# Hybrid recurrent decoder step: sample states stored between weight requests, and x and the first root placed first

## The chip, the cores and the metric

The kernel runs on one core of a Trainium2 chip. The metric is the time of one execution on the device, in microseconds (us); the numbers are medians over several runs.

## What is computed

One step of a decoder trunk of one layer with D = 1024, for a prompt of 512 tokens and a sample group of 8 sequences of 4 tokens. The kernel holds both as one tile of 544 columns. The reference, cut to what matters:

```python
mod = silu(c) @ ada_w + ada_b                    # adaLN, 6 x 1024 per group
h   = rms(x, norm1_w) * (1 + sc1) + sh1
proj = h @ w_in                                  # one projection for four mixers and their gates
# A: gated delta rule, B: HGRN2, C: SSD, D: mLSTM; each scans chunks and carries a state
o_a, S_gdn  = gated_delta(q, k, v, beta, logd, S_gdn)
o_b, S_hgrn = hgrn2(silu(q), kg, v, logf, S_hgrn)
o_c, S_ssd  = ssd_scan(C, B, x * dt, dt * -exp(a_log), S_ssd)      # then * silu(s_z)
o_d, C, n, m = mlstm(q, k, v, ig, lf, C, n, m)
y = (sum_n sigmoid(gate_n) * (branch_n @ w_branch_n)) @ w_out
x = x + gt1 * y
x = x + gt2 * (swiglu(rms(x, norm2_w) * (1 + sc2) + sh2))
return rms(x, final_norm_w), all new states of prompt and sample
```

The prompt's states start at zero. Those of the sample group are inputs, and their new values are outputs: `state_gdn`, `state_hgrn` and `state_mlstm_c` of 8 x 4 x 64 x 64 and `state_ssd` of 8 x 8 x 64 x 32 in float32, and some small ones.

## The kernel before, in words

Work goes to five instruction streams that wait for each other through semaphores. TensorE (PE) multiplies, ScalarE (ACT) copies PSUM out, takes exponentials and splits weights into a high part, VectorE (DVE) makes the low parts and the rest of the elementwise work, GpSimd (POOL) clears a few tiles, and SyncE (SP) asks for nearly every DMA, in one queue. SyncE's instructions run in program order, and one that waits for a semaphore holds up every request behind it.

**Opening.** SyncE requests c, the constants (`cst`, with the identity), x of the prompt and of the sample, four adaLN weights, small vectors, four more adaLN weights (L614 to L618 and after). TensorE first transposes c (stage `ct`); that needs the constants and c after its silu (stage `silc`, L1677). VectorE copies the result (`ctc`, L2007). Then TensorE transposes x in eight steps d; for each, ScalarE copies PSUM to `xT0` (L1687), VectorE squares (L2027) and TensorE sums the squares with a matrix of ones (`first_squares`, into banks 4 and 5). Between them it multiplies silu(c) with the first adaLN weights (`first_rows`) and turns the rows of the result into columns (`turn_rows`, 16 records in the profile for two of them, two records to a multiplication). The root, x's reciprocal norm, is a logarithm (L1697) and an exponential (L1699) on ScalarE, the stage `rs1`. After it VectorE normalises x (L2054), ScalarE makes high parts (L1725) and VectorE low parts (L2082) of h, for k = 0 to 7. Then VectorE makes the low part of the small gate weights (L2136).

**Mix stage.** 13 groups of `w_in` of 256 columns, two tiles each, are multiplied with h, each tile in four parts of 12 products. 22 tiles come early; the tiles 22 and 23 (SZ, written over Q_s, the SSD states of the sample) and 24 and 25 (MO) come after eight adaLN units. The weights lie in a ring of four slots, and `loads` numbers the requests: 0 to 3 and 15 to 30 are adaLN, 4 to 14 and 31, 32 mix, 33, 34 the two z groups. Request n waits until the work on request n - 4 is done. An adaLN unit v takes two requests, 15 + 2v and 16 + 2v (L634 for all of them). ScalarE copies each finished half tile out of PSUM (L1741) and makes the weights' high parts (`weights_high`, L1713); VectorE the low parts (`weights_low`, L2061).

**Chains.** Into this work the stages of three chains are woven: gdn (delta rule), hgrn, and rest (SSD, then mLSTM), each over the prompt's tiles and once over the sample's (t = NT). The order of all four is computed by `shared_order` from a table of costs, and fixed; each engine runs its part of it in that order. The stage `s_statec` finishes the sample's SSD states in Q_s, `g_statec` those of the delta rule in Q_g, `h_statec` those of HGRN2 in Q_h. They are sums made by VectorE (L2305). Q_s, Q_g and Q_h lie in `pj`, where later the tiles SZ, GZ and HG are written, so these writes wait for the stores, for instance

```python
if f == SZ:
    act.wait_ge(q_out["ssd"], 128)
act.activation(pj[:, f, h * HN:(h + 1) * HN], ps[:, h, 0:HN], ACT.Copy).then_inc(x_read, 1)
```

Q_c, the mLSTM states, lies where SSD's B and C were; it is fetched after `s_statec` (L729) and read by the sample's stage `m_out`. After the last of the 35 requests SyncE fetches Q_c, stores Q_s and S_s (the prompt's SSD state, L733), then Q_g and Q_h (L744). The gate weights follow.

Of the kernel before, what the change touches and what calls it, by code (L numbers as in the profile page):

```python
# [56 lines left out]
Y_BANK = [6, 0, 2, 6, 0]  # L57
ADA_ORDER = [0, 1, 4, 5, 2, 3, 6, 7]
# [312 lines left out]
def trunk(nc, A, O):  # L371

    ctx = ExitStack()
    with ctx:
# [237 lines left out]
        def _(sp):  # L612

            sp.dma_start(ctok(pj)[0:1, :], A["c_prompt"]).then_inc(d_c, 16)  # L614
            sp.dma_start(ctok(pj)[1:NB + 1, :], A["c_sample"]).then_inc(d_c, 16)
            sp.dma_start(cst[:, :], A["const"]).then_inc(d_cst, 16)
            sp.dma_start(xtok(pj), A["x_prompt"][0].rearrange("(a p) d -> p a d", p=P)).then_inc(d_x, 16)
            sp.dma_start(xstok(pj), A["x_sample"].rearrange("b t d -> (b t) d")).then_inc(d_x, 16)  # L618
# [79 lines left out]

            for n in range(R + 2, len(loads)):
# [6 lines left out]
                load(kind, n % R, idx)  # L706
                if n == 7:

                    pre.after(sp, 0, "xc")
                    sp.dma_start(x_out, part(0, KD * TA)).then_inc(d_xout, 16)  # L710
                    sp.dma_start(s_hist[0:3 * NB, :], A["state_ssd_conv"][0].rearrange("b k c -> (b k) c")).then_inc(d_hist, 16)
                    pre.after(sp, 0, "norm1")
                    sp.wait_ge(d_xout, 16)
                    sp.dma_start(g_hist[0:3 * NB, :], A["state_gdn_conv"][0].rearrange("b k c -> (b k) c")).then_inc(d_hist, 16)
# [11 lines left out]
            rest.after(sp, NT, "s_statec")  # L726
            for p in range(2):
                for q in range(2):
                    sp.dma_start(Q_c[q * DK:(q + 1) * DK, p], A["state_mlstm_c"][0, :, 2 * p + q].rearrange("b k v -> k b v")).then_inc(d_q["mlstm"], 16)  # L729
            stored_at = [0]  # L730

            def store(dst, src):
                sp.dma_start(dst, src).then_inc(stored, 16)  # L733
                stored_at[0] += 16

            def heads(dst, S):
                for p in range(2):
                    for q in range(2):
                        store(dst[2 * p + q], S[q * DK:(q + 1) * DK, p])

            def qheads(dst, S, name):
                for p in range(2):
                    for q in range(2):
                        sp.dma_start(dst[:, 2 * p + q].rearrange("b k v -> k b v"), S[q * DK:(q + 1) * DK, p]).then_inc(q_out[name], 16)  # L744
# [6 lines left out]
            for g in range(2):  # L751
                for j in range(4):
                    sp.dma_start(O[13][0, :, 4 * g + j].rearrange("b n v -> n b v"), Qs(Q_s)[g * DK:(g + 1) * DK, j]).then_inc(q_out["ssd"], 16)
                    store(O[5][0, 0, 4 * g + j], S_s[g * DK:(g + 1) * DK, j])
            gdn.after(sp, NT, "g_statec")
            qheads(O[10][0], Q_g, "gdn")
            hgrn.after(sp, NT, "h_statec")
            qheads(O[12][0], Q_h, "hgrn")
# [87 lines left out]
        def _(pe):  # L846
# [46 lines left out]
            for d in range(KD):  # L893
# [7 lines left out]
                if d in (1, 3, 5, 6):  # L901
                    first_rows((1, 3, 5, 6).index(d))
            first_squares(KD - 1).then_inc(x_summed, 1)
            turn_rows(0)
# [769 lines left out]
        def _(act):  # L1674
# [39 lines left out]

            for e in range(2):
                weights_high(0, e)
            act.wait_ge(x_summed, 1)
            rsqrt(pre, "rs1", two(rstd[:, :]), ps[:, 4:6, 0:HN], 1.0 / D)
# [269 lines left out]
        def _(dve):  # L1988
# [77 lines left out]
            for e in range(2):  # L2066
                weights_low(0, e)
            pre.after(dve, 0, "rs1")
            for k0 in (0, 4):
# [8 lines left out]
                for k in range(k0, k0 + 4):  # L2078
                    if k < k0 + 3:
# [3 lines left out]
                                             in1=h_hi[:, k, 0:T].bitcast(F32), op0=ADD, op1=SUB).then_inc(h_split, 1)  # L2083

# [862 lines left out]
```

## Time and profile before

| | us |
|---|---|
| median of 3 runs | 1234.47 |
| lowest and highest of them | 1229.53, 1234.59 |
| the profiled execution, its own time | 1237.73 |
| its span in the profile | 1235.9 |
| TensorE busy in it | 1162.4 |
| VectorE busy | 576.2 |
| ScalarE busy | 396.7 |

The profile is of one execution. Its times are counted from the start of the span, so the time of the program is the span and 1.8 us around it. Busy TensorE time is time with at least one matmul in flight; matmuls overlap, so the duration of one is longer than the distance between two starts. "PEclk" is the granted clock of TensorE as a share of 2.4 GHz; it has two levels, 1.2 and 2.4 GHz.

### The profile page before, as it was taken

The page shows a single profiled execution, that of the slowest core. Times are in us where ns is not written, and L with a number is a line of the kernel's source. Part 1 is how long each engine was busy: PE and PEld are TensorE (multiplying, and loading weights), DVE is VectorE, ACT ScalarE, POOL GpSimd, SP SyncE. Part 2 cuts the span into 40 slices and gives each one's busy share as a digit, 9 for nine tenths or more (in the row PEclk, how much of TensorE's full clock was granted, in tenths as well). Part 3 has the DMA queues.
Part 4 walks back from the last instruction along what each step waited for, and adds up shares of the span by engine and source line. Part 5 has one row for each costly group of instructions (what it writes and reads, how often), then busy time and mean ns, then how long its engine had stood idle before and what let it go on. Part 6 is the DMA issues. An engine that isn't in the chain of part 4 may idle for free. (4 is left out here: it accounts for less than half of the span.)

```text
span 1235.9 us, 26871 instructions
## 1 busy us (share of the span) xinstructions
PE 1162.4 (94%) x11789; PEld 1086.7 (88%) x11789; DVE 576.2 (47%) x1035; ACT 396.7 (32%) x546; POOL 11.6 (1%) x29
## 2 busy tenths in 40 slices
PE   6789989998989889999999999879999999999997
PEld 3589978887667879999999989779999999999996
DVE  1657867778578453523333354452222222453332
ACT  2535577521012136722222211242222232331121
POOL 0001100000000000000000000000000000000000
PEclk9889999998689799999999999989999999999998
DMA  9915311113646343363333231312323332232301
GB/s 297 278 49 118 109 36 37 37 37 105 206 139 170 75 102 79 84 141 86 85 86 86 86 86 39 97 35 69 102 75 95 88 82 81 70 94 72 94 1 73
DMA packets 191033, 116.76 MB, mean 94 GB/s; under 512 B 36650, under 2 KB 189351, under 8 KB 190678
## 3 DMA queue, kind: packets, MB, share of 16 engines
q1 hardware_dynamic: 190358, 115.16, 33.4%
q8 instruction: 79, 1.29, 0.4%
q0 software_dynamic: 576, 0.14, 0.1%
q14 instruction: 20, 0.16, 0.0%
HBM read 108.31 MB, written 6.96 MB: 93 GB/s over the span
## 5 line engine op out<-in xcount | busy, mean ns | idle before, releaser
L848 PE MATMUL ps<-high_parts,scr_parts 128*128 128x272 f32 x2848 | 549.8, 292 | 13.0 <-DVE hT_parts L2813 7.0
L848 PEld LDWEIGHTS ps<-high_parts,scr_parts 128*128 128x128 f32 x2848 | 452.8, 190 | 16.5 <-issue 7.7
L848 PE MATMUL ps<-hT_parts,scr_parts 128*128 128x272 f32 x1488 | 413.4, 290 | 0.0
L2710 DVE TENSOR_TENSOR scr_parts<-ring,scr_parts 128x1024 fp32r<-128x1024 f32 (+1 forms) x104 | 133.7, 1286 | 330.1 <-ACT scr_parts L1872 327.4
L848 PEld LDWEIGHTS ps<-hT_parts,scr_parts 128*128 128x128 f32 x1488 | 276.0, 189 | 0.0
L1872 ACT ACTIVATE scr_parts<-ring 128x1024 fp32r<-128x1024 f32 (+1 forms) x104 | 115.2, 1108 | 464.5 <-PE ps L848 464.1
L848 PE MATMUL ps<-pj_parts,scr_parts 128*128 128x272 f32 x992 | 166.5, 292 | 2.1 <-DVEq L2012 1.8
L848 PEld LDWEIGHTS ps<-pj_parts,scr_parts 128*128 128x128 f32 x992 | 140.5, 188 | 3.6 <-DVEq L2012 2.2
L848 PE MATMUL ps<-high_parts,ring_parts 128*128 128x272 f32 x416 | 124.2, 299 | 0.0
L848 PEld LDWEIGHTS ps<-high_parts,ring_parts 128*128 128x128 f32 x416 | 82.9, 199 | 0.1
L848 PE MATMUL ps<-scr 64*64 64x64 f32 (+6 forms) x2352 | 80.5, 233 | 2.4 <-DVEq L2012 1.3
L848 PEld LDWEIGHTS ps<-scr 64*64 64x64 f32 (+3 forms) x2352 | 63.6, 136 | 15.6 <-issue 7.0
L848 PE MATMUL ps<-high_parts,wx_hi 128*128 128x272 f32 x224 | 70.1, 313 | 6.1 <-ACT pj L1741 3.8
L848 PE MATMUL ps<-hT_parts,wx_hi 128*128 128x272 f32 x224 | 66.6, 297 | 0.0
L848 PE MATMUL ps<-high_parts,pj_parts 128*128 128x272 f32 x192 | 60.6, 315 | 3.3 <-ACT pj L1741 3.3
L848 PE MATMUL ps<-hT_parts,pj_parts 128*128 128x272 f32 x192 | 57.2, 298 | 0.0
L848 PEld LDWEIGHTS ps<-high_parts,wx_hi 128*128 128x128 f32 x224 | 44.5, 199 | 8.8 <-ACT pj L1741 4.6
L848 PEld LDWEIGHTS ps<-hT_parts,wx_hi 128*128 128x128 f32 x224 | 44.4, 198 | 0.0
L848 PEld LDWEIGHTS ps<-high_parts,pj_parts 128*128 128x128 f32 x192 | 38.2, 199 | 5.6 <-ACT pj L1741 3.9
L1741 ACT ACTIVATE pj<-ps 128x272 f32<-128x272 f32 x52 | 20.2, 389 | 66.9 <-PE ps L848 57.0
L2762 DVE TENSOR_TENSOR Rr<-pj,ps 128x544 f32<-128x544 f32 x16 | 11.5, 721 | 63.3 <-PE ps L848 63.0
L848 PE MATMUL ps<-pj 64*64 64x64 f32 (+2 forms) x308 | 37.8, 309 | 3.2 <-ACT scr L1853 3.2
(332 smaller groups left out, 1193.3 us busy)
## 6 DMA issues: line engine op xcount, KB each, us to landing
ring<-in_w_in_dram SPq DMA_DIRECT2D x62, 512.0 KB, 5.5
ring<-in_ffn_w_in_dram SPq DMA_DIRECT2D x44, 512.0 KB, 5.1
ring<-in_ada_w_dram SPq DMA_DIRECT2D x40, 512.0 KB, 6.1
ring<-in_ffn_w_out_dram SPq DMA_DIRECT2D x16, 384.0 KB, 3.6
ring<-in_ffn_w_out_dram SPq DMA_DIRECT2D x16, 320.0 KB, 4.1
pj<-in_ada_w_dram SPq DMA_DIRECT2D x8, 512.0 KB, 8.1
ring<-in_w_out_dram SPq DMA_DIRECT2D x8, 512.0 KB, 6.4
x_scratch<-scr SPq DMA_DIRECT2D x1, 2176.0 KB, 12.0
```

The source lines that it names most:

```text
L848: return pe.matmul(out, lhsT, rhs, start=start, stop=stop, skip_group_check=True)
L1741: act.activation(pj[:, f, h * HN:(h + 1) * HN], ps[:, h, 0:HN], ACT.Copy).then_inc(x_read, 1)
L1872: act.activation(hi, src, ACT.Copy).then_inc(w_split_hi, 1)
L2710: dve.tensor_tensor(lo, src, hi.bitcast(F32), SUB).then_inc(w_split, 1)
L2762: dve.tensor_tensor(two(Rr[:, :]), gate_t, lift, MUL).then_inc(lin_read, 1)
```

## The change

Four things are moved and nothing is added or left out:

- On SyncE, the fetch of Q_c and the stores of Q_s go out right behind weight request 23, after a wait for `s_statec`; the stores of Q_g behind request 28, after a wait for `g_statec`; those of Q_h behind request 32, after `h_statec`. The stores of S_s stay behind all requests.
- On SyncE, x is requested first and c last of the first five.
- On TensorE, `turn_rows(0)` comes ahead of the last `first_squares`. On ScalarE, the root `rs1` comes ahead of the high parts of mix tile 0.
- On VectorE, the low parts of mix tile 0 come behind the low parts of h for k = 1 and k = 3, no longer ahead of the wait for the root.

```diff
+SSD_OUT, GDN_OUT, HGRN_OUT = 23, 28, 32
...
+            sp.dma_start(xtok(pj), A["x_prompt"][0].rearrange("(a p) d -> p a d", p=P)).then_inc(d_x, 16)
+            sp.dma_start(xstok(pj), A["x_sample"].rearrange("b t d -> (b t) d")).then_inc(d_x, 16)
+            sp.dma_start(cst[:, :], A["const"]).then_inc(d_cst, 16)
             sp.dma_start(ctok(pj)[0:1, :], A["c_prompt"]).then_inc(d_c, 16)
             sp.dma_start(ctok(pj)[1:NB + 1, :], A["c_sample"]).then_inc(d_c, 16)
-            sp.dma_start(cst[:, :], A["const"]).then_inc(d_cst, 16)
-            sp.dma_start(xtok(pj), A["x_prompt"][0].rearrange("(a p) d -> p a d", p=P)).then_inc(d_x, 16)
-            sp.dma_start(xstok(pj), A["x_sample"].rearrange("b t d -> (b t) d")).then_inc(d_x, 16)
...
                 load(kind, n % R, idx)
+                if n == SSD_OUT:
+
+                    rest.after(sp, NT, "s_statec")
+                    for p in range(2):
+                        for q in range(2):
+                            sp.dma_start(Q_c[q * DK:(q + 1) * DK, p], A["state_mlstm_c"][0, :, 2 * p + q].rearrange("b k v -> k b v")).then_inc(d_q["mlstm"], 16)
+                    for g in range(2):
+                        for j in range(4):
+                            sp.dma_start(O[13][0, :, 4 * g + j].rearrange("b n v -> n b v"), Qs(Q_s)[g * DK:(g + 1) * DK, j]).then_inc(q_out["ssd"], 16)
+                if n == GDN_OUT:
+                    gdn.after(sp, NT, "g_statec")
+                    qheads(O[10][0], Q_g, "gdn")
+                if n == HGRN_OUT:
+                    hgrn.after(sp, NT, "h_statec")
+                    qheads(O[12][0], Q_h, "hgrn")
...
-            rest.after(sp, NT, "s_statec")
-            for p in range(2):
-                for q in range(2):
-                    sp.dma_start(Q_c[q * DK:(q + 1) * DK, p], A["state_mlstm_c"][0, :, 2 * p + q].rearrange("b k v -> k b v")).then_inc(d_q["mlstm"], 16)
...
             for g in range(2):
                 for j in range(4):
-                    sp.dma_start(O[13][0, :, 4 * g + j].rearrange("b n v -> n b v"), Qs(Q_s)[g * DK:(g + 1) * DK, j]).then_inc(q_out["ssd"], 16)
                     store(O[5][0, 0, 4 * g + j], S_s[g * DK:(g + 1) * DK, j])
-            gdn.after(sp, NT, "g_statec")
-            qheads(O[10][0], Q_g, "gdn")
-            hgrn.after(sp, NT, "h_statec")
-            qheads(O[12][0], Q_h, "hgrn")
...
+            turn_rows(0)
             first_squares(KD - 1).then_inc(x_summed, 1)
-            turn_rows(0)
             turn_rows(1)
...
+            act.wait_ge(x_summed, 1)
+            rsqrt(pre, "rs1", two(rstd[:, :]), ps[:, 4:6, 0:HN], 1.0 / D)
             for e in range(2):
                 weights_high(0, e)
-            act.wait_ge(x_summed, 1)
-            rsqrt(pre, "rs1", two(rstd[:, :]), ps[:, 4:6, 0:HN], 1.0 / D)
...
             first_modulation(0)
-            for e in range(2):
-                weights_low(0, e)
             pre.after(dve, 0, "rs1")
...
                                              in1=h_hi[:, k, 0:T].bitcast(F32), op0=ADD, op1=SUB).then_inc(h_split, 1)
+                    if k in (1, 3):
+                        weights_low(0, k // 2)
```

SyncE, the weight requests of the mix stage and what follows them, two DMAs to a request. Before:

```order
L634 DMA ring<-in_w_in_dram 128x4x256 x8
L634 DMA ring<-in_ada_w_dram 128x4x256 x32
L634 DMA ring<-in_w_in_dram 128x4x256 x8
L729 DMA pj<-in_state_mlstm_c_dram 64x8x64 x4
L753 DMA out_dram<-pj 64x8x32
L733 DMA out_dram<-S_s 64x32
```

And now:

```order
L635 DMA ring<-in_ada_w_dram 128x4x256 x18
L729 DMA pj<-in_state_mlstm_c_dram 64x8x64 x4
L732 DMA out_dram<-pj 64x8x32 x8
L635 DMA ring<-in_ada_w_dram 128x4x256 x10
L714 DMA out_dram<-pj 64x8x64 x4
L635 DMA ring<-in_ada_w_dram 128x4x256 x4
L635 DMA ring<-in_w_in_dram 128x4x256 x4
L714 DMA out_dram<-pj 64x8x64 x4
L635 DMA ring<-in_w_in_dram 128x4x256 x4
L703 DMA out_dram<-S_s 64x32 x8
```

The fetch and the stores that stood behind the last of the `w_in` requests now stand between the adaLN requests: 12 DMAs behind 23, 4 behind 28, 4 behind 32.

ScalarE, in the opening, from the last copies of x on. Before:

```order
L1713 ACTIVATE wx_hi<-ring 128x512 x2
L1697 ACT_TABLE_LOAD
L1697 ACTIVATE rstd<-ps,colp 128x544
L1699 ACT_TABLE_LOAD
L1699 ACTIVATE rstd<-rstd 128x544
L1681 ACTIVATE scr<-ps 128x512
```

And now:

```order
L1705 ACT_TABLE_LOAD
L1705 ACTIVATE rstd<-ps,colp 128x544
L1707 ACT_TABLE_LOAD
L1707 ACTIVATE rstd<-rstd 128x544
L1721 ACTIVATE wx_hi<-ring 128x512 x2
L1689 ACTIVATE scr<-ps 128x512
```

The two high parts of mix tile 0 (`wx_hi`) have gone behind the root.

VectorE, in the opening, from the end of the first modulation on. Before:

```order
L1992 TENSOR_TENSOR coef<-coef,vt 128x36
L2061 TENSOR_TENSOR ring_parts<-ring,wx_hi 128x4x128 x2
L1992 TENSOR_TENSOR hT<-scr,rstd 128x4x32
L1992 TENSOR_TENSOR hT<-hT,coef 128x4x32
L2050 TENSOR_TENSOR hT<-hT,mod 128x4x32
```

And now, from the low part of h for k = 1 on (`hT_parts` is the low part, `hT` the normalised x):

```order
L2088 SCALAR_TENSOR_TENSOR hT_parts<-hT,mod,high_parts 128x512
L2069 TENSOR_TENSOR ring_parts<-ring,wx_hi 128x4x128
L2062 SCALAR_TENSOR_TENSOR hT<-scr,coef,rstd 128x512
L2088 SCALAR_TENSOR_TENSOR hT_parts<-hT,mod,high_parts 128x512 x2
L2069 TENSOR_TENSOR ring_parts<-ring,wx_hi 128x4x128
```

The low parts of the weights (`ring_parts`), which stood ahead of the first instruction that needs the root, now stand one behind k = 1 and one behind k = 3.

## Rows read from the trace of the kernel before

**Rows 1.** The page, part 1: busy us, share of the span, instructions.
```profile
PE 1162.4 (94%) x11789; PEld 1086.7 (88%) x11789; DVE 576.2 (47%) x1035; ACT 396.7 (32%) x546; POOL 11.6 (1%) x29
```
**Rows 2.** Windows of 5 us: busy us (instructions) of each engine, PEclk, DMA share, GB/s.
```profile
395.00:400.00 5.00, 4.94 (x109) 4.41 (x109) 4.29 (x9) 0.00 (x0) 0.00 (x0) 1.00 0.27 42
400.00:405.00 5.00, 0.35 (x3) 0.13 (x2) 2.11 (x5) 0.90 (x3) 0.00 (x0) 0.84 0.34 58
405.00:410.00 5.00, 4.66 (x31) 3.94 (x32) 2.82 (x8) 1.70 (x4) 0.00 (x0) 0.50 0.87 189
```
**Rows 3.** Waits, 385 to 410 us: us in total, times, longest.
```profile
PE ps L848 <- ACTq L1777: 5.0, 1, 5.0
```
**Rows 4.** Timeline of ScalarE: start, us, instruction, [idle before <- releaser].
```profile
404.10 0.40 ACT L1741 ACTIVATE pj<-ps 128x272 f32<-128x272 f32 x1 [9.78 <-DMA out_dram<-pj]
```
**Rows 5.** Timeline of TensorE, 396 to 414 us.
```profile
405.34 0.69 PE L848 MATMUL ps<-S_g,scr 64*64 64x64 f32 x8 [4.99 <-ACTq L1777]
...
407.50 0.60 PE L848 MATMUL ps<-high_parts,pj_parts 128*128 128x272 f32 x1
...
410.16 0.33 PE L848 MATMUL ps<-hT_parts,pj_parts 128*128 128x272 f32 x1
...
413.43 0.44 PE L848 MATMUL ps<-Rr,cst 96*32 96x32 f32 x8
```
**Rows 6.** Timeline of SyncE's queue, 310 to 405 us: issues, not transfers.
```profile
314.41 2.47 SPq L634 DMA_DIRECT2D ring<-in_ada_w_dram  x4
...
382.49 6.21 SPq L729 DMA_DIRECT2D pj<-in_state_mlstm_c_dram  x4
388.74 1.62 SPq L753 DMA_DIRECT2D out_dram<-pj  x1
...
401.85 0.60 SPq L753 DMA_DIRECT2D out_dram<-pj  x1
```
**Rows 7.** Timeline of VectorE: last sums of the states in Q_s and Q_g.
```profile
288.88 0.42 DVE L2305 TENSOR_TENSOR pj<-pj,ps 128x256 f32<-128x256 f32 x1
...
325.46 1.22 DVE L2305 TENSOR_TENSOR pj<-pj,ps 128x1024 f32<-128x1024 f32 x1
```
**Rows 8.** TensorE reads request 24; landing of the weight requests, 190 to 392 us.
```profile
345.71 1.93 PE L848 MATMUL ps<-ring,scr 128*32 128x256 f32 x16
...
DMA to landing us min/median/max: 3.5/5.5/9.4
```
**Rows 9.** The opening, timelines of SyncE, ScalarE, TensorE and VectorE.
```profile
1.49 0.36 SPq L616 DMA_DIRECT2D cst<-in_const_dram  x1
...
3.05 1.06 ACT L1677 ACTIVATE pj<-pj 9x1024 f32<-9x1024 f32 x1 [1.02 <-DMA pj<-in_c_sample_dram]
...
5.76 1.02 PE L852 MATMUL ps<-cst,pj 9*128 9x9 f32 x8 [5.76 <-DMA cst<-in_const_dram]
12.65 2.64 PE L852 MATMUL ps<-cst,pj 128*128 128x128 f32 x10 [5.88 <-DMA pj<-in_x_sample_dram]
...
6.81 0.23 DVE L2007 COPY scr<-ps 128x72 f32<-128x72 f32 x1 [2.07 <-PE ps L852]
```
**Rows 10.** From the last sums of squares: TensorE, ScalarE, VectorE.
```profile
34.66 1.18 PE L848 MATMUL ps<-hT,cst 128*128 128x272 f32 x4 [0.44 <-DVE hT L2027]
35.68 1.85 PE L848 MATMUL ps<-cst,scr 128*128 128x9 f32 x16
...
36.66 1.15 ACT L1713 ACTIVATE wx_hi<-ring 128x512 fp32r<-128x512 f32 x2 [2.83 <-DMA ring<-in_w_in_dram]
...
39.12 0.71 ACT L1697 ACTIVATE rstd<-ps,colp 128x544 f32<-128x544 f32 x1
...
39.31 1.30 DVE L2061 TENSOR_TENSOR ring_parts<-ring,wx_hi 128x512 fp32r<-128x512 f32 x2
41.90 0.29 DVE L1992 TENSOR_TENSOR hT<-scr,rstd 128x128 f32<-128x128 f32 x1 [1.29 <-ACTq L1700]
...
57.92 1.22 DVE L2136 TENSOR_TENSOR scr_parts<-scr,scr_parts 128x1024 fp32r<-128x1024 f32 x1
```

More of the change, by code:

```diff
@@ L697, in _, with store, heads, qheads @@
             sp.dma_start(hrow[64:68, 0:NB * 5:5], A["state_mlstm_m"][0].rearrange("b h -> h b")).then_inc(d_st, 16)
+            stored_at = [0]
+            def store(dst, src):
+                sp.dma_start(dst, src).then_inc(stored, 16)
+                stored_at[0] += 16
+            def heads(dst, S):
+                for p in range(2):
+                    for q in range(2):
+                        store(dst[2 * p + q], S[q * DK:(q + 1) * DK, p])
+            def qheads(dst, S, name):
+                for p in range(2):
+                    for q in range(2):
+                        sp.dma_start(dst[:, 2 * p + q].rearrange("b k v -> k b v"), S[q * DK:(q + 1) * DK, p]).then_inc(q_out[name], 16)
             for n in range(R + 2, len(loads)):
@@ L706, in _ @@
                 load(kind, n % R, idx)
+                if n == SSD_OUT:
+                    rest.after(sp, NT, "s_statec")
+                    for p in range(2):
+                        for q in range(2):
+                            sp.dma_start(Q_c[q * DK:(q + 1) * DK, p], A["state_mlstm_c"][0, :, 2 * p + q].rearrange("b k v -> k b v")).then_inc(d_q["mlstm"], 16)
[8 more added lines that the diff above has]
+                    qheads(O[12][0], Q_h, "hgrn")
                 if n == 7:
@@ L724, in _ @@
                             sp.dma_start(Qs(Q_s)[g * DK:(g + 1) * DK, j], A["state_ssd"][0, :, 4 * g + j].rearrange("b n v -> n b v")).then_inc(d_q["ssd"], 16)
-            rest.after(sp, NT, "s_statec")
-            for p in range(2):
-                for q in range(2):
-                    sp.dma_start(Q_c[q * DK:(q + 1) * DK, p], A["state_mlstm_c"][0, :, 2 * p + q].rearrange("b k v -> k b v")).then_inc(d_q["mlstm"], 16)
[L730 to L744, printed above, removed]
             def lift_weights(d):
```

## The prediction

> **What bounds the kernel now.** I read the page's busy times first: TensorE is busy for 94% of the span [rows 1]. Time can be won only where TensorE stands still or runs at its lower clock. Next I read the table of 5 us windows for a stretch where both happen. One bears on this change: in 400 to 405 us TensorE is busy for 0.35 us of 5, and in the next window the granted clock is 0.50, its lower level of 1.2 GHz [rows 2]. Then the waits from 385 to 410 us: TensorE waited 5.0 us for ScalarE [rows 3]. The timeline of ScalarE says for what it waited itself, 9.78 us: the copy of mix tile SZ out of PSUM starts at 404.10, when `q_out["ssd"]` is full (L1740), because the tile is written over Q_s. Behind it in ScalarE's queue stands the copy of the delta rule's sk product (L1774, L1775), which TensorE needs for its next instruction [rows 4]. Last the timelines of SyncE's queue and of VectorE: the eight SSD stores are requested from 388.74 to 401.85 [rows 6], yet the state they store was final at 289.3, its last addition at 288.88 being 0.42 us long [rows 7]. They are late only because SyncE asks for them after every weight of the mix stage. So this wait is an order of requests, not work.
>
> **Part 1: SSD stores and mLSTM fetch behind weight request 23.** Requests 23 and 24 go out together at 314.41, four DMAs in 2.47 us, two to a request [rows 6]. Request 23 is thus out at 314.41 + 2.47/2 = 315.6, 26 us after the state is final, so the new wait on the chain costs nothing. Then follow 4 fetches of Q_c, 6.21 us before, and 8 stores. Between the first and the last store 13.1 us passed for 15 requests, of which 7 were of S_s [rows 6]; taking S_s at about the rate of the rest, the eight cost between 5 us (0.60 each, the last row's) and 14 us. I take 9. The stores leave SyncE at about 315.6 + 6.2 + 9 = 331 and land by about 334. Nothing reads Q_s until ScalarE's copy, some 60 us later. The 9.8 us wait goes whole.
>
> What is it worth? ScalarE would read the first half of SZ when TensorE has finished it, at about 396.4, then do the sk copies when their product is there, about 398.7, well before TensorE's 400.35. TensorE's idle time of 4.99 us before 405.34 [rows 5] goes: **-5.0 us**. The work after it ran slowly: 2.16 us from 405.34 to 407.50, then the first eleven of 36 mix matmuls at (410.16 - 407.50)/11 = 0.24 us each; the following 25 took (413.43 - 410.16)/25 = 0.13 us [rows 5]. With no gap in front, I let this work run at the upper clock: 2.16/2 + 11 x (0.24 - 0.13) = **-2.3 us**, bounded by 0 if the clock falls anyway and by 2.4 if the whole 4.8 us from 405.34 to 410.16 ran in half the time. Against a gain here: what is late next is VectorE, which is busy in that stretch with the mLSTM and HGRN2 stages up to 402.3; but TensorE has 36 mix matmuls (4.5 us) to do before it needs those, so I charge nothing, and at most 2 us (402.3 less 400.35) if that cover is gone.
>
> What is queued behind the 12 moved DMAs is request 24, at about 331 instead of 315.6, and it lands 5.5 us later by the median, 9.4 at most [rows 8]: 336 to 341. TensorE reads that slot at 345.71 [rows 8]. Requests 25 and 26 were free at 327 and are read after 350. Cost 0, with 5 to 10 us to spare.
>
> **Part 2: GDN and HGRN2 stores behind requests 28 and 32.** Their states are final at 326.7 and 357.6 (the first by [rows 7]), the requests go out after 347 and 372. Four stores each cost SyncE some 2.7 us, before the next weight requests that wait for the adaLN work anyway. Nobody waited for these stores before. They cost 0, and spare 0. The S_s stores stay behind, in time nobody needs.
>
> **Part 3: the opening, x placed first.** Before, c was there at 3.05, the constants at 5.76, and x released TensorE at 12.65 [rows 9]. The chain is: c, silu (1.06), eight transposes of c that also wait for the constants (1.02), a copy on VectorE (0.23), and only then the transposes of x. Now c is the last of the five requests. The bytes are the same and the queue hands them over in its order, so the last lands where x landed, 12.55, less some 0.7 us, since the first large request was issued third, at 1.49 [rows 9], and is now issued first: 11.8. c is tiny and needs less of the tail, so I take 11.5. Then 11.5 + 1.06 + (7.2 - 5.76, transposes and copy with their handovers) gives 14.0: x starts **+1.4 us** later, bounded by +0.4 (c early, the constants alone gate at 11.6) and +2.5 (c at 12.55). A negative value is excluded: the constants also come behind x now. In the trace, the small x_sample request landed behind the large one, in order. The Trainium skill, page "DMA: Bandwidth & Descriptors", section "Queues, rings and completion order", says completion is not first in, first out for one issuing engine: a small DMA on few rings need not wait for the others' rings. By that rule c would land ahead of the constants, this term would be +0.4 and the whole sum -8.3; no row here shows a small request overtake a large one.
>
> **Part 4: the root first.** Before, ScalarE waited 2.83 us for weights, split them from 36.66, and only then took the logarithm at 39.12; VectorE began to normalise at 41.90, 2.78 us after [rows 10]. The sums were complete at 34.66 + 1.18 = 35.84. Now four of the eight turned rows (1.85/2 = 0.92) come ahead of the last sums, which fills the 0.44 us they waited for VectorE, so the sums end at 36.3; the table load runs while ScalarE waits. VectorE may begin at 36.3 + 2.8 = 39.1: **-2.8 us**; the modulation, whose copy waits for the turned rows, is ready about then (39.2). But the low parts of the weights, 1.30 us of VectorE that lay in its wait for the root [rows 10], now lie among its normalising: **+1.3**, and ScalarE's split in front of the first high part costs about +0.1. VectorE has no idle time from 41.90 to the small weights' low part at 57.92, for which TensorE waits [rows 10]; so its shift is the opening's: +1.4 - 2.8 + 1.3 + 0.1 = **0.0 us**, from -1.0 to +1.1. TensorE starts its first mix products earlier but stalls on the same VectorE work.
>
> **The sum.** -5.0 - 2.3 + 0.0 = -7.3 us, 0.6%. The sum is made against the profiled execution, 1237.7 us with a span of 1235.9, which gives 1230.4 there. The median of the runs shown is 3.3 us lower, 1234.47, and the same difference gives 1227.2. About 0.5%, 6.2 us, is what a measurement of this kernel can tell from no change.
>
> **The rivals.**
> 1. Only the idle time comes back. The clock falls to 1.2 GHz also elsewhere, where TensorE does many tiny products rather than stand still, so the slow stretch may remain; or TensorE meets VectorE's work 2 us on. For it: the stages around 400 us are full of 64-column products. Against it: the clock was 1.00 up to the gap and fell in it [rows 2]. With an opening of +0.5: -5.0 + 0.5 = -4.5, 1230.0; within 0.5%.
> 2. The opening costs more than the root gives back: c lands last of all (+2.5), and the low parts are not hidden. -7.3 + 1.1 = -6.2, 1228.3, and with part of rival 1, 1231.5. For it: x_sample came after x, in order.
> 3. Slower: weight request 24 is late. The 12 moved DMAs stand in front of it on SyncE, and the eight stores write runs of 128 bytes. It decides once SyncE is held beyond 345.71 - 5.5 = 340.2, that is 24 us instead of 15; each us beyond is one of TensorE's, since its products are in program order. To end 0.5% slower it must lose 7.3 + 6.2 = 13.5 us: held for 38 us. Then about 1241. Against it: before, the same 12 and eight more took 401.85 + 0.6 - 382.49 = 20 us [rows 6]. The same page, in its specifications, wants at least 512 bytes for full rate and has smaller ones read, modified and written; were the stores twice as long for it, SyncE would be held 24 us, just at the edge and with no loss. The time before already includes that effect.
> 4. The change does not do what it says: the SSD stores were not what ScalarE waited for. Then only the opening is left, 1234.5. Against it: the wait ends 1.65 us after the last of them was issued (404.10 less 401.85 + 0.60) [rows 4, 6].
>
> **How the numbers follow.** The forecast (wait and slow stretch gone, opening even) has 0.57, rival 1 0.20, rival 2 0.13 (half of it over the 0.5%), rival 3 0.05, rival 4 0.05. Predicted is the forecast, 1227.2. Its own range is 1225 to 1229.5. Downwards I go to 1223.5, for an opening of -1.0 and a faster run like the lowest shown; upwards to 1232, which takes in rivals 1 and 2. Faster by over 0.5%: 0.57 + 0.06 = 0.63; within 0.5%: 0.20 + 0.07 + 0.05 = 0.32; slower: 0.05.
>
> **What would show it.** Right: ScalarE's copy of SZ has no DMA wait; TensorE has no gap of 5 us after the last products of tile SZ, and a clock near 1.00 behind them; the SSD stores are issued near 322 to 331 and request 24 before 335. The transposes of x start at 13.5 to 14.5, VectorE's low part of the small weights ends at 59.1, give or take 1. Wrong: a TensorE gap before the adaLN rows near 345; a slow stretch at 395 to 400 with no gap ahead of it; x transposed before 12.65 or after 15; a gain with another place than the stretch at 400 us.

## The result, and the profile after

| | before | after |
|---|---|---|
| median of 20 runs each, us | 1238.0 (1229.53 to 1243.23) | 1228.9 (1222.54 to 1236.39) |
| ratio to before, 95% interval | 1 | 0.9935 [0.9916, 0.9953] |
| profiled execution: span, us | 1235.9 | 1221.8 |
| mean granted clock of TensorE | 0.961 | 0.969 |

The kernel is 0.65% faster, some 8.0 us; the interval reaches from 5.8 to 10.4 us. (The medians are 9.1 us apart, the means of the same runs 8.1; I go by the ratio and its interval.) The forecast was a gain of 7.3 us. The two traces differ by 14.1 us; why that is more than the times show is taken up with the repeated traces below.

The page, part 1, of the kernel after (busy us, share of the span, instructions). Against [rows 1] the counts are the same, and TensorE is busy for 9.8 us less though it does the same work: it runs for less time at the lower clock. Not all of that is the change's; the repeated traces below show how much differs by chance.

```profile
PE 1152.6 (94%) x11789; PEld 1079.3 (88%) x11789; DVE 576.0 (47%) x1035; ACT 396.9 (32%) x546; POOL 11.9 (1%) x29
```

The windows of 5 us of the kernel after where [rows 2] had a TensorE busy for 0.35 us of 5 and then a clock of 0.50:

```profile
395.00:400.00 5.00, 4.80 (x66) 4.17 (x57) 4.56 (x8) 2.42 (x5) 0.00 (x0) 1.00 0.01 3
400.00:405.00 5.00, 5.00 (x82) 4.67 (x83) 3.06 (x11) 0.71 (x2) 0.00 (x0) 1.00 0.00 0
405.00:410.00 5.00, 5.00 (x112) 4.56 (x111) 2.89 (x9) 1.03 (x2) 0.00 (x0) 1.00 0.13 14
```

All that TensorE still waits for from 385 to 410 us (in total, times, longest). The wait of [rows 3] is gone, and what is left is VectorE, for which the kernel before waited 1.3 us in the same window:

```profile
PE ps L856 <- DVEq L2020: 1.6, 3, 1.2
PE ps L860 <- DVEq L2020: 0.2, 1, 0.2
```

ScalarE in the kernel after: the copy of tile SZ, which waited 9.78 us for a DMA [rows 4], now waits for TensorE's products alone, and so does the sk copy behind it. (Line numbers are 8 higher than before: L1749 was L1741.)

```profile
392.92 0.40 ACT L1749 ACTIVATE pj<-ps 128x272 f32<-128x272 f32 x1 [1.73 <-PE ps L856]
...
395.58 0.38 ACT L1782 ACTIVATE scr<-ps 128x256 f32<-128x256 f32 x1 [2.27 <-PE ps L856]
```

To measure the stretch apart from all that comes ahead of it, I take a landmark on TensorE ahead of it, the start of the last 32 adaLN products (one row of the timeline, x32), and read forward. Timeline of TensorE, kernel before, those rows that do not stand in [rows 5]:

```profile
377.64 1.93 PE L848 MATMUL ps<-ring,scr 128*32 128x256 f32 x32
...
405.96 1.03 PE L852 MATMUL ps<-cst,pj 128*32 128x128 f32 x4
406.92 0.64 PE L848 MATMUL ps<-Er,cst 96*64 96x32 f32 x8
```

And kernel after:

```profile
374.50 1.93 PE L856 MATMUL ps<-ring,scr 128*32 128x256 f32 x32
...
397.17 0.45 PE L856 MATMUL ps<-S_g,scr 64*64 64x64 f32 x8
397.82 0.61 PE L860 MATMUL ps<-cst,pj 128*32 128x128 f32 x4 [0.20 <-DVEq L2020]
398.36 0.42 PE L856 MATMUL ps<-Er,cst 96*64 96x32 f32 x8
398.71 0.39 PE L856 MATMUL ps<-high_parts,pj_parts 128*128 128x272 f32 x1
...
403.44 0.44 PE L856 MATMUL ps<-Rr,cst 96*32 96x32 f32 x8
```

From the landmark to the `S_g` products it was 27.70 us and is 22.67: 5.03 us of idle time gone. From there to the `Rr` products it was 8.09 and is 6.27: 1.82 us of slow stretch gone. Together 6.85 us.

SyncE's queue in the kernel after (a row is a group of issues), with TensorE's read of request 24 as its last row. The fetch of Q_c and the eight SSD stores hold SyncE from 316.07 to 326.13, 10.1 us; request 24 leaves at 326.13 and is read at 343.74, without a wait. Before it was read at 345.71 [rows 8].

```profile
316.07 3.40 SPq L729 DMA_DIRECT2D pj<-in_state_mlstm_c_dram  x4
319.51 6.58 SPq L732 DMA_DIRECT2D out_dram<-pj  x8
326.13 20.77 SPq L635 DMA_DIRECT2D ring<-in_ada_w_dram  x10
346.94 6.20 SPq L714 DMA_DIRECT2D out_dram<-pj  x4
...
381.03 7.13 SPq L703 DMA_DIRECT2D out_dram<-S_s  x8
```
```profile
343.74 1.07 PE L856 MATMUL ps<-ring,scr 128*32 128x256 f32 x16
```

The opening in the kernel after (SyncE, ScalarE, TensorE, VectorE; compare [rows 9, 10]): c arrives last, x is transposed from 14.53 in place of 12.65, VectorE normalises from 39.59 in place of 41.90, and reaches the small weights' low part at 56.91 in place of 57.92.

```profile
2.71 0.28 SPq L619 DMA_DIRECT2D pj<-in_c_sample_dram  x1
...
11.83 1.05 ACT L1685 ACTIVATE pj<-pj 9x1024 f32<-9x1024 f32 x1 [9.80 <-DMA pj<-in_c_sample_dram]
...
13.03 0.99 PE L860 MATMUL ps<-cst,pj 9*128 9x9 f32 x8 [13.03 <-ACT pj L1685]
14.53 2.61 PE L860 MATMUL ps<-cst,pj 128*128 128x128 f32 x10 [0.51 <-DVEq L2020]
...
39.59 0.29 DVE L2000 TENSOR_TENSOR hT<-scr,rstd 128x128 f32<-128x128 f32 x1 [0.31 <-ACTq L1708]
...
56.91 1.22 DVE L2144 TENSOR_TENSOR scr_parts<-scr,scr_parts 128x1024 fp32r<-128x1024 f32 x1
```

### The profile page after: what moved, and what is told of

Read it like the earlier page. It is cut to its first block and busy times, and to the rows that moved or that the text cites. A ratio compares the mean times of both kernels' runs of the same rounds, so it can differ in the third digit from the quotient of the medians.

```text
span 1221.8 us, 26871 instructions
## 1 busy us (share of the span) xinstructions
PE 1152.6 (94%) x11789; PEld 1079.3 (88%) x11789; DVE 576.0 (47%) x1035; ACT 396.9 (32%) x546; POOL 11.9 (1%) x29
## 5 line engine op out<-in xcount | busy, mean ns | idle before, releaser
L2770 DVE TENSOR_TENSOR Rr<-pj,ps 128x544 f32<-128x544 f32 x16 | 11.5, 721 | 63.3 <-PE ps L856 63.1
L1749 ACT ACTIVATE pj<-ps 128x272 f32<-128x272 f32 x52 | 20.2, 389 | 56.4 <-PE ps L856 56.1
```

The source lines that it names most:

```text
L2770: dve.tensor_tensor(two(Rr[:, :]), gate_t, lift, MUL).then_inc(lin_read, 1)
```

## The experiments

My theory: the gain is ScalarE's wait for the SSD stores and the slow stretch behind it, and the opening is even. Its rivals: the gain comes from the opening; the GDN and HGRN2 stores take part in it; the stores in front of request 24 can cost what they bring. The first four kernels take the change apart. They ran on one chip, the next four on a second and the last two on a third, each group beside runs of the kernel before on its chip.

**The stores alone.** The kernel after with the opening of the kernel before (order of the five requests, sums behind the turned rows, root behind the high parts, low parts together).

```
...
+            first_squares(KD - 1).then_inc(x_summed, 1)
             turn_rows(0)
-            first_squares(KD - 1).then_inc(x_summed, 1)
...
+            for e in range(2):
+                weights_high(0, e)
             act.wait_ge(x_summed, 1)
             rsqrt(pre, "rs1", two(rstd[:, :]), ps[:, 4:6, 0:HN], 1.0 / D)
-            for e in range(2):
-                weights_high(0, e)
...
```

> Only the stores and the fetch are moved; the opening is that of before. Theory: they carry the whole gain, 7 us (ratio near 0.994), all of it in the stretch from the mix tile SZ to the first product of the sample's mLSTM broadcast: ScalarE's copy of SZ has no DMA wait, TensorE no gap of 5 us behind the last product of SZ, and the granted clock is 1.00 there. Rival: the opening carries a third or more; then this kernel gains 5 us or less (ratio 0.996 or above) though the stretch looks the same.

Measured: 1227.6 us, ratio 0.9934 [0.9901, 0.9967]: the whole gain without the opening. Its opening is that of before to 0.01 us at VectorE (41.89 and 57.92). The same stretch, landmark to `S_g`, takes 22.65 us, with no gap.

**The opening alone.** The kernel before with those opening edits.

```
+            sp.dma_start(xtok(pj), A["x_prompt"][0].rearrange("(a p) d -> p a d", p=P)).then_inc(d_x, 16)
+            sp.dma_start(xstok(pj), A["x_sample"].rearrange("b t d -> (b t) d")).then_inc(d_x, 16)
+            sp.dma_start(cst[:, :], A["const"]).then_inc(d_cst, 16)
             sp.dma_start(ctok(pj)[0:1, :], A["c_prompt"]).then_inc(d_c, 16)
...
```

> Only the opening is changed; stores and fetch go out after all weights as before. Theory: x starts 1.9 us later, the root 2.3 us earlier, the end of the small weights' low part comes 1 us earlier, and the time is within 0.2% of before. The wait of nearly 10 us of ScalarE is there again. Rival: the opening carries a third or more of the gain, 3 us (ratio 0.9975 or below).

Measured: 1235.49 us, ratio 1.0012 [0.9981, 1.0043]: nothing that can be told, though the interval alone would leave room for a loss of 5 us or a gain of 2. x starts at 14.51, as expected, but VectorE normalises from 40.47 and reaches the small low part at 57.80, 0.1 us before the kernel before and not 1 us: my instants were those of the first trace of the kernel after. The wait stands as before, here first ScalarE's, then TensorE's:

```profile
404.93 0.40 ACT L1741 ACTIVATE pj<-ps 128x272 f32<-128x272 f32 x1 [9.28 <-DMA out_dram<-pj]
```
```profile
406.17 0.69 PE L848 MATMUL ps<-S_g,scr 64*64 64x64 f32 x8 [4.47 <-ACTq L1777]
```

**c first, the rest as after.** Only the five requests go back to the order c, constants, x.

```
-            sp.dma_start(xtok(pj), A["x_prompt"][0].rearrange("(a p) d -> p a d", p=P)).then_inc(d_x, 16)
-            sp.dma_start(xstok(pj), A["x_sample"].rearrange("b t d -> (b t) d")).then_inc(d_x, 16)
-            sp.dma_start(cst[:, :], A["const"]).then_inc(d_cst, 16)
             sp.dma_start(ctok(pj)[0:1, :], A["c_prompt"]).then_inc(d_c, 16)
...
+            sp.dma_start(cst[:, :], A["const"]).then_inc(d_cst, 16)
+            sp.dma_start(xtok(pj), A["x_prompt"][0].rearrange("(a p) d -> p a d", p=P)).then_inc(d_x, 16)
```

> As the changed kernel, but the first requests in the old order: c, constants, x. Theory: x last was never the trouble; c is needed ahead of x. The transposes of x start at 12.6 instead of 14.5, the root and all behind it 1 to 1.9 us earlier than in the changed kernel, and the time is 1 to 2 us below it (about 0.992 of before). Rival: the later start of x is covered by the weight products or by a shorter slow stretch of TensorE's clock, and the time of the end of the small weights' low part (58.1 in the changed kernel) does not move.

Measured: 1229.03 us, ratio 0.9927 [0.9898, 0.9956]. x starts at 11.97, VectorE normalises from 37.97 and reaches the small low part at 55.45. So x first costs time and the root first gives it back; the instants say so, and the 1 to 2 us that I expected in the time cannot be told from the kernel after by the ratio.

**The SSD stores alone moved.** The GDN and HGRN2 stores go back behind the last request.

```
-                if n == GDN_OUT:
-                    gdn.after(sp, NT, "g_statec")
-                    qheads(O[10][0], Q_g, "gdn")
...
```

> As the changed kernel, but the stores of the delta rule's and HGRN2's states are put back behind all weights. Theory: nobody waits for them at either place, the time is that of the changed kernel within 1 us. Rival: at the old place they stand in front of the gate weights and of the writes of GZ and HG, and cost 1 us or more; or at the new place they delay weight requests, and taking them away gains as much.

Measured: 1231.73 us, ratio 0.9953 [0.9927, 0.9979]. The ratio is 0.0018, 2.2 us, above that of the kernel after, where I expected 1 us at most; the intervals overlap by about half. The trace says that the stretch is the same, 28.94 us from the landmark to `Rr`, against 28.94 in the kernel after. So the GDN and HGRN2 stores bring nothing there; that they bring 1 or 2 us in another place is not excluded by the times. This execution does come late to the landmark (384.26), but at least 3.9 us of that lie ahead of the read of request 24 (351.57, against 343.74 and 347.67 in two traces of the kernel after), where the two kernels do not differ.

**The SSD stores last, but not among others.** One number changed.

```
-SSD_OUT, GDN_OUT, HGRN_OUT = 23, 28, 32
+SSD_OUT, GDN_OUT, HGRN_OUT = 34, 28, 32
```

> The kernel after, with the fetch of Q_c and the eight SSD stores requested right behind the last weight request (34) and ahead of the S_s stores, in place of behind request 23; the GDN and HGRN2 stores stay where the change has them. Theory A (ScalarE's copy of SZ waits for the last of the eight stores to land, whatever stands around them; a pause of TensorE costs its own length and a slow stretch behind it): the fetch and stores leave SyncE from about 381 to 391 and land by 393 to 394, ScalarE's copy, free to go at about 393 to 396, waits 0 to 1 us for a DMA and not 9.8, TensorE has a gap of at most 1 us at 397, no slow stretch behind it, and the ratio to the kernel before is that of the kernel after, 0.992 to 0.996. Theory B (it is the interleaving with S_s and the late place together; the place behind request 23 is needed): a gap of 3 to 5 us stays, ratio 0.997 to 1.001.

Measured: 1232.34 us, ratio 0.9953 [0.9929, 0.9977]. SyncE's queue, then ScalarE, then TensorE:

```profile
389.68 5.97 SPq L729 DMA_DIRECT2D pj<-in_state_mlstm_c_dram  x4
395.69 8.23 SPq L732 DMA_DIRECT2D out_dram<-pj  x8
```
```profile
405.59 0.40 ACT L1749 ACTIVATE pj<-ps 128x272 f32<-128x272 f32 x1 [5.62 <-DMA out_dram<-pj]
```
```profile
400.10 0.91 PE L856 MATMUL ps<-scr 64*64 64x64 f32 x24 [0.85 <-issue]
...
406.83 0.45 PE L856 MATMUL ps<-S_g,scr 64*64 64x64 f32 x8 [0.27 <-ACTq L1785]
```

ScalarE waits 5.62 us for the DMA, where I had expected at most 1. My instants were those of another trace: this execution reached the landmark at 383.27, 8.8 us later than the kernel after, the w_in requests and so the stores moved with it, and the eight took 8.23 us to issue. TensorE's gap was as expected, 0.27 us. From the landmark to `S_g` it is 23.56 us, 0.90 more than in the kernel after, and not all of that is ScalarE's: TensorE also stood still for 0.85 us ahead of 400.10, before ScalarE's copy could matter to it, and for that wait the profile shows no releaser. The last product ahead of `S_g` starts at 406.28, and in the kernel after `S_g` follows that product by 0.22 us; here it follows by 0.55. So a wait of 5.6 us on ScalarE cost TensorE 0.3 us, and 0.6 came from elsewhere. ScalarE's copy was near the path even so. Over the four traces in which ScalarE's copy waits for a DMA, `S_g` starts 1.24 us after it, to 0.01: 404.10 and 405.34 before, 403.55 and 404.78 in its repetition, 404.93 and 406.17, 405.59 and 406.83. So it delays `S_g` only if it starts later than 22.66 - 1.24 = 21.4 us behind the landmark. In the kernel after it starts 392.92 - 374.50 = 18.4 us behind it, with 3.0 us to spare. And the two pauses of 0.85 and 0.27 us had no slow stretch behind them (`S_g` to `Rr` 6.00 us, against 6.27), while those of 4.3 to 5.0 us had one (8.09 to 8.27).

**Request 24 held back.** The kernel after with 24 more stores of the same shape, to a scratch tensor, behind the eight SSD stores.

```
...
+                    for m in range(24):
+                        g, j = m // 4 % 2, m % 4
+                        store(junk[m].rearrange("b n v -> n b v"), Qs(Q_s)[g * DK:(g + 1) * DK, j])
```

> The kernel after, with 24 more stores of the same shape (64 KB each, runs of 128 bytes) to a scratch tensor of their own between the eight SSD stores and weight request 24. Rival 3's price: each further store costs SyncE some 0.8 us (6.58 us for eight in the trace of the kernel after), so SyncE is held 10 + 20 = 30 us and request 24 leaves at about 346 in place of 326. It lands 5.5 us later by the median, at 351 to 355; TensorE, which reads it at 343.7 in the kernel after, stands still for 8 to 12 us before the adaLN rows, with a slow stretch behind. If rival 3's arithmetic holds (each us beyond 340 costs one us of TensorE), the run is 8 to 13 us slower than the kernel after: ratio to the kernel before 0.999 to 1.005. If later slack absorbs the delay (TensorE waits later for other things anyway), ratio 0.993 to 0.996. A slow stretch that costs more than I charge would give over 1.006.

Measured: 1241.06 us, ratio 1.0033 [1.001, 1.0056], slower than the kernel before. SyncE's queue, TensorE, and three windows of 5 us (the columns as in [rows 2]):

```profile
329.78 18.67 SPq L704 DMA_DIRECT2D junk<-pj  x24
348.50 10.45 SPq L636 DMA_DIRECT2D ring<-in_ada_w_dram  x10
```
```profile
346.88 1.12 PE L860 MATMUL ps<-pj 64*64 64x64 f32 x30
354.18 1.93 PE L860 MATMUL ps<-ring,scr 128*32 128x256 f32 x16 [6.18 <-DMA ring<-in_ada_w_dram]
```
```profile
345.00:350.00 5.00, 3.00 (x88) 2.81 (x86) 4.58 (x9) 0.35 (x1) 0.00 (x0) 0.50 0.45 71
350.00:355.00 5.00, 0.82 (x8) 0.40 (x12) 0.96 (x2) 0.00 (x0) 0.00 (x0) 0.50 1.04 332
355.00:360.00 5.00, 5.00 (x48) 3.02 (x40) 1.62 (x5) 0.80 (x2) 0.00 (x0) 0.68 1.10 349
```

Two windows of the repeated trace of the kernel after, which reads request 24 at 347.67 without a wait:

```profile
345.00:350.00 5.00, 5.00 (x100) 3.61 (x99) 4.66 (x8) 0.45 (x2) 0.00 (x0) 0.50 0.00 0
350.00:355.00 5.00, 5.00 (x44) 2.78 (x42) 3.98 (x10) 0.46 (x2) 0.00 (x0) 0.88 0.86 266
```

A store costs SyncE 18.67/24 = 0.78 us; request 24 leaves at 348.50 and lands 5.7 us later. TensorE stands still for 6.18 us, less than the 8 to 12 I expected. The clock was at its lower level of 1.2 GHz already before the pause, in both traces; without the pause it is at 0.88 from 350 to 355, with it at 0.50 there and at 0.68 from 355 to 360. From the read of request 24 to the landmark it is 35.32 us here and 30.3 to 32.7 in all eleven other traces: 2.6 to 5.1 us of slow work on top of the pause. So the 6.2 us of pause cost 8.8 to 11.3 us, an estimate of 1.4 to 1.8 us for each; the spans of this trace and the repeated one differ by 10.1, the ratios by 0.0095, which is 11.8 us. Rival 3's mechanism is real, and its price is higher than one us for one.

**The constants split.** c, then the first 384 columns of the constants, then x, then the rest of them, for which TensorE waits before `turn_rows(0)`.

```
...
+            sp.dma_start(cst[:, 0:K_NEGS], A["const"][:, 0:K_NEGS]).then_inc(d_cst, 16)
             sp.dma_start(xtok(pj), A["x_prompt"][0].rearrange("(a p) d -> p a d", p=P)).then_inc(d_x, 16)
             sp.dma_start(xstok(pj), A["x_sample"].rearrange("b t d -> (b t) d")).then_inc(d_x, 16)
+            sp.dma_start(cst[:, K_NEGS:K_N], A["const"][:, K_NEGS:K_N]).then_inc(d_cst2, 16)
...
+            pe.wait_ge(d_cst2, 16)
             turn_rows(0)
```

> The kernel after, with c first, then only the first 384 columns of the constants (identity, block of 64, ones), then x, and the rest of the constants last; TensorE waits for that rest before it first turns the rows. If what starts x is the bytes ahead of x in the queue: the constants behind x are some 1 us of transfer, so x starts at 10.5 to 11.5 in place of 14.5 (after) and 12.0 (c first, then all constants), VectorE's root at 36.5 to 37.5 and its small low part near 54 to 55, so the run is 0.5 to 1 us below the run with c first and 2 to 3 us below the kernel after: ratio to the kernel before 0.990 to 0.993. If the start of x is bound by the landing of x itself and not by what stands ahead of it: no change to c first, 0.9925 to 0.9935.

Measured: 1227.24 us, ratio 0.9926 [0.9898, 0.9954]. The start of x and of the normalising (37.39) came as expected, the small low part did not. TensorE's timeline, then ScalarE's, then VectorE's:

```profile
11.14 2.64 PE L862 MATMUL ps<-cst,pj 128*128 128x128 f32 x10 [5.92 <-DMA pj<-in_x_sample_dram]
...
40.10 1.89 PE L858 MATMUL ps<-pj,scr 128*32 128x256 f32 x16 [2.57 <-DMA pj<-in_ada_w_dram]
43.12 1.94 PE L858 MATMUL ps<-pj,scr 128*32 128x256 f32 x16 [1.12 <-DMA pj<-in_ada_w_dram]
```
```profile
45.12 0.60 ACT L1692 ACTIVATE scr<-ps 128x512 f32<-128x512 f32 x1 [4.12 <-PE ps L858]
```
```profile
46.36 1.41 DVE L2091 SCALAR_TENSOR_TENSOR hT_parts<-hT,mod,high_parts 128x512 fp32r<-128x512 f32 x2 [2.86 <-ACT high_parts L1736]
...
57.77 1.22 DVE L2147 TENSOR_TENSOR scr_parts<-scr,scr_parts 128x1024 fp32r<-128x1024 f32 x1
```

TensorE reaches the adaLN products before their weights are there and waits 2.57 and 1.12 us, and then does sixteen in 1.9 us and not 1.07. ScalarE's copy of these products waits 4.12 us for them, the high part of h stands behind that copy, and VectorE waits 2.86 us for the high part. From the start of the normalising to the small low part it is 20.38 us here and 17.30 to 17.48 in the other traces with the root first. In this trace the next bound of the opening is the landing of the adaLN weights, and the small low part comes later (57.77) than where x starts at 12 (55.45, 56.28). It is one trace.

**The kernel after, a second time**, unchanged.

> The kernel after, unchanged, once more, for a second trace and for a comparison with the split constants on the same chip. Expected: ratio to the kernel before 0.9935 within its interval (0.992 to 0.995); the same instants of the opening within 0.2 us (x starts at 14.5, VectorE normalises from 39.6); no gap of TensorE at 400; but a time lost below the full clock that differs by several us from the 37.9 us of the first trace, most of it between 300 and 380 us, where the change does nothing. If instead the 37.9 us come back here, the change itself raises the clock before 380 us.

Measured: 1230.05 us, ratio 0.9938 [0.9911, 0.9965], span 1228.0, clock 0.965. Span times what the clock is short of 1, the time lost at the lower clock, is 43.0 us here, 37.9 in the first trace, 48.2 before. So two executions of one program differ by 6.2 us, some 5 of it by the clock. Summed over windows of 5 us, the difference from 300 to 380 us is 4.9 us (15.3 against 10.4), as expected, and ahead of 300 it is 1.7 the other way. The opening was not the same to 0.2 us as expected: VectorE normalises from 41.12, not 39.59. TensorE's timeline of this trace, and a window:

```profile
17.75 2.18 PE L856 MATMUL ps<-hT,cst 128*128 128x272 f32 x4 [0.27 <-DVE hT L2035]
...
23.02 1.40 PE L856 MATMUL ps<-hT,cst 128*128 128x272 f32 x4
...
24.96 1.18 PE L856 MATMUL ps<-hT,cst 128*128 128x272 f32 x4
```
```profile
14.00:20.00 6.00, 5.22 (x22) 3.36 (x25) 1.68 (x3) 1.37 (x4) 0.00 (x0) 1.00 1.09 348
```

In the first trace the 1.18 us were reached already in the second group:

```profile
21.71 1.18 PE L856 MATMUL ps<-hT,cst 128*128 128x272 f32 x4
```

**c first, a second time.**

> The kernel after with c, the constants and x in the old order, a second time. It is to tell apart whether the 2 us by which this kernel led the kernel after come from the opening. If they do: x starts at 12.0 give or take 0.3, VectorE normalises from 38.0 and its low part of the small weights begins at 55.5 give or take 0.3, in place of 58.0 (mean of six traces with x first); ratio 0.992 to 0.994. If 55.45 was chance (TensorE's first products after its long rest run slowly for a length that differs between executions): 56.5 to 58. From the adaLN read behind request 32 to the Rr products 28.94 us, as in every trace with the stores moved.

Measured: 1227.02 us, ratio 0.9944 [0.9916, 0.9973]. x at 12.46, normalising from 38.91, small low part at 56.28: later than I gave for the first case and just short of the second, 1.8 us ahead of the mean of the six traces with x first. The opening with c first is better by 1.8 to 2.6 us at VectorE, but two runs of it (0.9927, 0.9944) beside two of the kernel after (0.9935, 0.9938) give the same time. I claim no faster version.

**The kernel before, a second time.**

> The kernel before, unchanged, for a second trace of it. Theory (the span of the first trace of before, 14.1 us over that of after, holds chance of the clock beside the change): from the adaLN read behind request 32 to the Rr products 35.5 to 35.8 us again, but the rest behind Rr 818 to 821 us as in all nine traces of the other kernels, and not 822.5; the gap of TensorE at 400 us is again 4.5 to 5.0. If the rest is again 822 or more, the change has an effect behind 413 us that I have not found, though the opening alone (819.5) speaks against it.

Measured: 1237.23 us in one run, span 1235.4, the gap 4.34 us. From the landmark to `Rr` it is 35.17, a little under the 35.5 I had given; behind `Rr` 822.5 us again, which is the other case of my expectation. So I looked on with a second landmark, the `Vr` products, 10 to 12 us behind `Rr`, with another fall of the clock just ahead of them. All twelve traces, in us:

| | landmark | to `S_g` | to `Rr` | `Rr` to `Vr` | rest |
|---|---|---|---|---|---|
| before | 377.64 | 27.70 | 35.79 | 12.46 | 810.0 |
| before, again | 377.72 | 27.06 | 35.17 | 12.46 | 810.1 |
| opening alone | 378.97 | 27.20 | 35.47 | 12.28 | 807.2 |
| after | 374.50 | 22.67 | 28.94 | 10.47 | 807.9 |
| after, again | 379.50 | 22.65 | 28.93 | 12.08 | 807.5 |
| stores alone | 377.79 | 22.65 | 28.94 | 11.73 | 808.1 |
| c first | 375.35 | 22.66 | 28.95 | 11.60 | 808.7 |
| c first, again | 377.26 | 22.65 | 28.95 | 11.91 | 810.8 |
| SSD stores alone | 384.26 | 22.65 | 28.94 | 10.46 | 807.6 |
| SSD stores last | 383.27 | 23.56 | 29.56 | 10.25 | 808.3 |
| request 24 held | 389.50 | 22.67 | 28.94 | 11.74 | 807.9 |
| constants split | 373.25 | 22.66 | 28.93 | 10.24 | 808.5 |

The column to `Rr` is the cleanest result of the study. It is 35.17 to 35.79 in the three traces with the stores unmoved (mean 35.48) and 28.93 to 28.95 in the eight with them behind request 23: 6.54 us by the means. `Rr` to `Vr` is 12.40 against 11.16 on the mean of all nine others, and every one of them is shorter. But the nine fall into two groups, four with 10.2 to 10.5 and five with 11.6 to 12.1. Beside the five the difference is 0.6 us, and three traces with the stores unmoved cannot say that the short length is closed to them. So this stretch adds 0.6 to 1.2 us, and that the change does it is not shown. Together 7.1 to 7.8 us, beside 8.0 by the times. The rest scatters by 3 us on both sides of the change and can be put down to neither. So of the 14.1 us between the first two traces 6.85 is the stretch, 1.99 the one behind it, 3.14 lies ahead of the landmark and 2.1 in the rest. The last two cannot be put down to the change: the repeated trace of the kernel after comes to the landmark 1.9 us later than before did, not 3.1 earlier.

## Why the prediction was right, and where a term was off

- **Part 1, idle time, -5.0.** Right: 5.03 in the pair of traces, 4.4 to 5.0 in all. The name of the waiter, its releaser and its place were right, and the stores alone bring the whole gain.
- **Part 1, slow stretch, -2.3.** Measured -1.82. The step that was mis-sized is "2.16/2": the three groups from `S_g` to the first mix matmul took 2.16 us and now 398.71 - 397.17 = 1.54, not 1.08. Small products that hand over to one another, with a wait of 0.20 us for VectorE among them, do not take half the time at twice the clock. The mix matmuls did as I had it: 5.93 before, 403.44 - 398.71 = 4.73 after, -1.2. Over all traces the stretch gained 6.5, not 7.3. What I did not look at is the next slow stretch, shorter by 0.6 to 1.2 us. That the whole came so near, 7.1 to 7.8 by the traces, is partly luck: the two errors nearly cancel.
- **What is late next.** I charged nothing for VectorE, and the stretch has no wait of over 1.2 us for it (1.8 us in all from 385 to 410, against 1.3 before). Right.
- **Request 24.** I gave it 331; it left at 326.13, since the eight stores took 6.58 us and not 9, and the fetch 3.40 and not 6.2. It cost nothing, as predicted, with more to spare than I gave.
- **Part 2, GDN and HGRN2 stores, 0.** Right in the stretch. The issue time was mis-sized: four took 6.20 us, not 2.7. The 2.7 was the rate at the old place, eight in 5.41 us. Most of the time sat where SyncE would have waited for a free slot: requests 29 and 30 leave 9.2 us behind the read of request 24 in the kernel before, 9.1 with the SSD stores alone moved, and 9.4 to 11.1 behind it in the traces with the GDN stores moved (but for that with request 24 held). In the two traces of the kernel after TensorE waits for no DMA from 343 to 385 us.
- **Part 3, x later by 1.4.** Too small. The six traces with x first start it at 14.35 to 14.87, mean 14.65; the five with c, all constants and x start it at 11.97 to 12.65, mean 12.32: +2.3, just inside my +2.5. A third of the error is the row I counted from: 12.65 is the latest of those five. The rest is the chain: in the first trace c landed at 11.83, not 11.5, and silu to x took 2.70, not 2.50. c, issued last of the five and nine rows long, was what ScalarE waited for in all six. The Trainium skill's page "DMA: Bandwidth & Descriptors", section "Queues, rings and completion order", says that completion is not first in, first out for one issuing engine; I had read from it that c could land ahead of the constants, with a term of +0.4. No trace here shows that: x then had to start near 13.1, and the earliest start is 14.35. The page only denies that the order is kept; it does not say that a small late request lands first, so the traces do not speak against it.
- **Part 4, root -2.8, low parts +1.3.** From the start of x to the normalising it was 29.15 to 29.88 us in three traces and is 25.06 to 26.45 in nine, -3.3 by the means. From there to the small low part 16.02 became 17.32, between 17.30 and 17.48 in eight traces (all but the split constants): +1.30, as worked out from the duration of the two instructions.
- **The opening's sum, 0.0.** Measured +0.2 at VectorE (mean 58.04 of six traces, against 57.84 of three) and 1.0012 [0.9981, 1.0043] by the times. Right, but partly by luck: two of its terms were off by 0.9 and 0.5 in opposite directions.
- **The rivals.** 1 (only idle time) falls: the slow stretch went. 2 (the opening costs over 1 us) falls by the instants at VectorE, though c did land last of all; the times of the opening alone would not exclude it. 3 (request 24 late) does not happen here, but the run with 24 more stores shows it. Its threshold was right: SyncE was held 348.50 - 317.67 = 30.8 us and TensorE paused for 6.2, so the pause would begin at 24.6, and I gave 24. Its price was not: I counted one us of TensorE per us, and it was 1.4 to 1.8. By that estimate 0.5% slower than before would come at 24 us and 13.5/1.8 to 13.5/1.4 more, 31.5 to 34 us held, not at 38. 4 (not ScalarE's wait) falls.

## What to carry to other kernels

Where an engine waits for a store of data that was final 100 us earlier, the wait is an order of requests: move the store to the place where its data is ready, and first work out how long the request behind it can wait (here 10 us were used of 343.74 - 5.5 - 316.07 = 22). Cost the pause together with the slow stretch behind it: TensorE pauses of 4.3 to 5.0 us cost 6.2 to 6.9, two of 0.85 and 0.27 cost no more than their own length. To compare two traces use landmarks on one engine on both sides of the changed place: spans of one program differed by 6 us here, the stretch between landmarks by 0.02 where no pause lay in it, and by 0.6 where one did.

## What was not expected of the hardware

- TensorE's first products after its long wait for x run at half their later rate although the granted clock of that window is 1.00: four matmuls of 128x272 in 2.18 us at 17.75, in 1.18 from 24.96. The full rate came at 21.7 in one trace of the kernel and after 23 in another, and that alone moved the whole opening by 1.2 us. What decides it stays open. The column itself may be what is wrong there: it says 1.00 also for 5 to 10 us, in which TensorE does nothing, while 2.18 against 1.18 us is about the ratio seen elsewhere between windows at 0.50 and at 1.00 (sixteen adaLN products in 1.93 and in 1.07). No run here decides it.
- The time that SyncE takes to issue the same stores differs by place: eight of 64 KB in a row took 6.25 to 8.23 us over the traces, four of 128 KB between the weight requests 4.99 to 7.25, and eight of 128 KB behind all of them 5.41 to 5.79. What sets it is not shown.
- Why two executions of one program lose 38 and 43 us at the lower clock, most of the difference between 300 and 380 us, was not found.
